# The adaLN rows of the first normalisation computed by halves of the channels in a hybrid RWKV-7 / MLA / MoE block

## What is computed

```python
mod = jax.nn.silu(c) @ w_ada[l] + b_ada[l]                       # (1, 6 * 1024)
sh_m, sc_m, gt_m, sh_f, sc_f, gt_f = jnp.split(mod, 6, axis=-1)
h = modulate(rmsnorm(x, g_norm_mix[l]), sh_m, sc_m)              # h * (1 + sc_m) + sh_m
z = h @ w_in[l]
...
w_log = -jax.nn.softplus(-(w0 + jnp.tanh(zw) @ w_decay_up)) - 0.5
a = jax.nn.sigmoid(a0 + za @ w_a_up)
```

## Time and profile before

| | us |
|---|---|
| median of 3 runs | 1513.24 |
| lowest and highest run | 1509.96, 1517.48 |
| profiled execution, its own time | 1519.26 |
| its span | 1517.4 |
| PE busy | 1384.3 (91%) |
| DVE busy | 761.0 (50%) |
| ACT busy | 492.4 (32%) |
| POOL busy | 313.4 (21%) |

### The profile page before, as it was taken

The page is one execution under the profiler, slowest core; times in us unless marked ns, Lnnn a source line. Parts: engine busy times, 40 slices in busy tenths (PEclk is TensorE's granted clock), DMA queues, the critical chain, the costliest instruction groups (busy, mean ns, idle before and its releaser), DMA issues. The chain is left out here.

```text
span 1517.4 us, 32870 instructions
## 1 busy us (share of the span) xinstructions
PE 1384.3 (91%) x14305; PEld 997.9 (66%) x14305; DVE 761.0 (50%) x1139; ACT 492.4 (32%) x891; POOL 313.4 (21%) x327
## 2 busy tenths in 40 slices
PE   3899999986999998799989999999996799999996
PEld 2687777735899998677767888787885333332332
DVE  3715676766677665445647555656455422111111
ACT  4433232263344443444435444413111111111110
POOL 0002221205556552011110000000000123332323
PEclk8899999997999999899999999999997699999998
DMA  9761322270000001750003113514227899999992
GB/s 373 272 187 45 91 76 63 80 269 2 4 4 4 4 11 39 208 201 15 15 15 153 56 56 110 195 46 167 84 83 275 352 345 399 382 402 376 398 364 56
DMA packets 74956, 238.20 MB, mean 157 GB/s; under 512 B 12216, under 2 KB 37304, under 8 KB 58048
## 3 DMA queue, kind: packets, MB, share of 16 engines
q1 hardware_dynamic: 63872, 219.31, 38.7%
q0 software_dynamic: 10944, 16.82, 4.6%
HBM read 207.74 MB, written 51.40 MB: 171 GB/s over the span
## 5 line engine op out<-in xcount | busy, mean ns | idle before, releaser
L3050 PE MATMUL ps<-gu,xT 128*32 128x512 f32 x1296 | 178.3, 609 | 5.0 <-DMA gu<-w_e_up 3.5
L3266 DVE TENSOR_TENSOR sg<-sg,ps 128x256 f32<-128x256 f32 x25 | 10.5, 421 | 206.6 <-ACT sg L3136 206.6
L3050 PEld LDWEIGHTS ps<-gu,xT 128*32 128x32 f32 x1296 | 46.8, 112 | 98.9 <-issue 95.3
L2937 POOL DMA_INDIRECT out<-YTM,home x48 | 75.2, 1566 | 169.3 <-DVE YTM L3275 162.0
L354 PE MATMUL ps<-hh,wr_h 128*128 128x512 f32 x224 | 94.0, 420 | 4.5 <-DVE hl L350 3.8
L355 PE MATMUL ps<-hl,wr_h 128*128 128x512 f32 x224 | 89.4, 399 | 0.0
L356 PE MATMUL ps<-hh,wr_l 128*128 128x512 f32 x224 | 89.4, 399 | 0.0
L3068 PE MATMUL ps<-dn,hidT 128*32 128x512 f32 x648 | 86.7, 592 | 0.5 <-ACT hidT L3140 0.5
L2117 DVE TENSOR_REDUCE nmax<-ps 128x1 f32<-128x896 f32 (+4 forms) x64 | 45.8, 753 | 72.3 <-PE ps L2015 71.7
L2955 POOL MEMSET xg<- 128x3072 f32 x1 | 2.7, 2657 | 366.5 <-PE ps L2442 366.5
L1285 POOL TENSOR_TENSOR off<-mats,cst 128x256 f32<-128x256 f32 x80 | 66.7, 851 | 50.9 <-PE ps L1707 50.6
(11 more groups left out here) (440 smaller groups left out, 3432.8 us busy)
## 6 DMA issues: line engine op xcount, KB each, us to landing
gu<-w_e_gate SPq DMA_DIRECT2D x29, 1024.0 KB, 17.4
gu<-w_e_up SPq DMA_DIRECT2D x29, 1024.0 KB, 23.5
dn<-w_e_down SPq DMA_DIRECT2D x29, 1024.0 KB, 18.0
wbuf<-w_ada SPq DMA_DIRECT2D x16, 1024.0 KB, 12.9
wbuf<-w_ada SPq DMA_DIRECT2D x16, 512.0 KB, 4.6
wraws<-w_gates SPq DMA_DIRECT2D x16, 512.0 KB, 4.9
wr<-w_rwkv SPq DMA_DIRECT2D x14, 512.0 KB, 3.6
qk_cols<-YTM SPq DMA_DIRECT2D x8, 768.0 KB, 5.3
```

The source lines that it names most:

```text
L2937: pool.indirect_dma_start(out=out[0], out_offset=bass.IndirectOffsetOnAxis(ap=col.bitcast(u32), axis=0), in_=yo[:, buf], in_offset=None, b ...
L3050: last = nc.tensor.matmul(ps[part, GB[b]], xT[:, b, k, part], gu[expert(m, c_) % WB][:, :, k], start=(k == 0), stop=(k == KD - 1))
```

## The change

**Rows of the first modulation.** A new class `HalfRows` takes the place of `Rows` for the first pair (not for `rows4` and `rows2`). Channels are split in two halves of 512 columns. Half h has the shift columns in strip 32h and the scale columns in strip 64 + 32h of its own PSUM bank (6 or 5), so a piece is 512 KB and costs two matmul calls on two strips 64 apart; there are 16 pieces. The bias comes into PSUM as a product of a row of ones with the bias row (`biased`). ACT copies the shift strip out (`shift_row`), DVE the scale strip with the gain (`scale_row`).

**Order.** All eight tiles of `x` are loaded first (tile 7 into the space of `zm`), then bias and gains, then half 0 of the rows, the first two weight tiles, half 1, and the rest. Only the identity and one row of the constants come early. Squares of tiles 1 and 3 move to DVE, roots go by two tiles. PE starts with half 0's bias product, runs half 0's pieces among the transposes, then channel block 0, half 1's bias product and first four pieces, block 1, the other four pieces, block 2, the second turn of the rows, and blocks 3 to 7.

**Phases 2 and 3.** `up_projections` has the token halves outside and the two row groups inside; its weights are loaded some 200 us earlier, and the table `sel` is waited for together with them. The four stores of `rows2` move to the start of phase 3, and DVE waits for its own last bias add instead. The setting up of `S` and `headrk` moves from DVE to POOL, behind `prepare(0)`.

```diff
+        class HalfRows:
...
+            def part(self, h, a):
+                return slice(64 * a + 32 * h, 64 * a + 32 * h + 32)
...
+            def load_bias(self, sp):
+                sp.dma_start(self.bias[0:1], b_ada[:, 0:2 * D]).then_inc(self.b_in, 16)
+                for h in range(2):
+                    sp.dma_start(self.gains[self.part(h, 1)],
+                                 g_norm_mix[:, h * 512:(h + 1) * 512].broadcast_to([32, 512])).then_inc(self.b_in, 16)
...
+            def biased(self, pe, h):
+                pe.wait_ge(self.b_in, 48)
+                for a in range(2):
+                    nc.tensor.matmul(ps[self.part(h, a), self.banks[h]], C("ones")[0:1, 0:32],
+                                     self.bias[0:1, a * D + h * 512:a * D + (h + 1) * 512], start=True, stop=False,
+                                     skip_group_check=True)
...
+            def products(self, pe, h, k):
...
+                pe.wait_ge(self.w_in[h][k], 16)
+                for a in range(2):
+                    m = nc.tensor.matmul(ps[self.part(h, a), self.banks[h]], self.crep[:, k], self.piece(h, k)[:, a],
+                                         start=False, stop=(k == KD - 1), skip_group_check=True)
+                m.then_inc(self.mm, 1)
...
+                    squares(0)
+                    roots(0)
+                    squares(2)
+                    roots(1)
+                    squares(4)
+                    turned(0)
+                    squares(5)
+                    roots(2)
+                    for t in (1, 2):
+                        turned(t)
+                    for t in (6, 7):
                         squares(t)
...
+                    pe.wait_ge(const_in, 32)
+                    rows0.biased(pe, 0)
+                    for t in range(NT):
+                        row_transposes(t)
+                        if t >= NT - 3:
+                            for k in range(2 * (t - NT + 3), 2 * (t - NT + 3) + 2 if t < NT - 1 else KD):
+                                rows0.products(pe, 0, k)
+                    row_columns(0)
+                    channel(0)
+                    rows0.biased(pe, 1)
+                    for k in range(CT):
+                        rows0.products(pe, 1, k)
+                    channel(1)
+                    for k in range(CT, KD):
+                        rows0.products(pe, 1, k)
+                    channel(2)
+                    row_columns(1)
+                    for k in range(3, KD):
+                        channel(k)
...
-                    rows2.store(sp, 1)
...
-                        for j, (w, src, done) in enumerate(((wup[0:64], Z(WA)[0:64], dec),
-                                                            (wup[64:128], Z(WA)[64:128], a_done))):
-                            if c_:
-                                pe.wait_ge(done, c_)
-                            for n in range(2):
+                        for n in range(2):
+                            for j, (w, src, done) in enumerate(((wup[0:64], Z(WA)[0:64], dec),
+                                                                (wup[64:128], Z(WA)[64:128], a_done))):
+                                if c_ and n == 0:
+                                    pe.wait_ge(done, c_)
...
+                    nc.gpsimd.memset(S[:], 0.0).then_inc(init, 1)
+                    for c_ in range(CT):
+                        nc.gpsimd.tensor_scalar(headrk[:, c_], C("heads"), PC("r_k", c_), None, ALU.mult)\
+                          .then_inc(init, 1)
```

More of the change, by code:

```diff
@@ L536, in _, with roots @@
                     nc.scalar.activation(csig[:], ccol[:], ACT.Sigmoid).then_inc(c_sig, 1)
+                    act.wait_ge(const_in, 32)
+                    nc.scalar.activation(mcol[:, 0, 0, 0:1], C("ident")[:, 0:1], ACT.Sqrt)
                     def squares(t):
[L539 to L546, removed]
+                        act.wait_ge(x_in[t], 16)
+                        n = sum(i not in ON_DVE for i in range(t))
+                        if n:
+                            act.wait_ge(ssq, n)
+                        nc.scalar.activation(tmp[:], rows_of(t), ACT.Square, accum_out=ss[:, t:t + 1]).then_inc(ssq, 1)
+                    def roots(two):
+                        cols = slice(2 * two, 2 * two + 2)
+                        act.wait_ge(rstd, 2 * two + 1)
                         nc.scalar.activation(rs[:, cols], rs[:, cols], ACT.Sqrt).then_inc(root, 1)
@@ L553, in turned @@
                           .then_inc(xn_a, 1)
-                    for t in range(4):
+                    squares(0)
[9 more added lines that the diff above has]
+                    for t in (6, 7):
                         squares(t)
[L556 to L559, removed]
+                    roots(3)
+                    for t in range(3, NT):
                         turned(t)
-                    squares(XT)
-                    roots(1)
-                    for t in range(4, NT):
-                        turned(t)
+                    rows0.shift_row(act, 0)
                     for c_ in range(2):
                         weights(c_, 16)
-                    act.wait_ge(mcol_s, 1)
                     act.wait_ge(xn_a, NT)
@@ L721, in _ @@
                         low_part(hl[:, k], xn(k), hh[:, k]).then_inc(h_lo, 1)
+                    squares(1)
+                    roots(0)
+                    for t in (0, 1):
+                        scale_rows(t)
+                    squares(3)
+                    roots(1)
+                    for t in (2, 3):
+                        scale_rows(t)
+                        turned(t - 2)
+                    turned(2)
+                    roots(2)
+                    for t in (4, 5):
+                        scale_rows(t)
+                    for t in (3, 4):
+                        turned(t)
+                    roots(3)
+                    for t in (6, 7):
+                        scale_rows(t)
+                    for t in (5, 6, 7):
+                        turned(t)
+                    rows0.scale_row(dve, 0)
+                    columns(0)
+                    weights(0, 1)
+                    dve.wait_ge(mcol_s, 1)
+                    dve.wait_ge(xn_a, NT)
+                    dve.wait_ge(xn_d, NT)
+                    modulated(0)
+                    weights(1, 2)
+                    for k in range(1, CT):
+                        modulated(k)
+                    nc.vector.memset(zT[:, 0:2, 0:1], 0.0).then_inc(zero, 1)
+                    rows0.scale_row(dve, 1)
+                    columns(1)
+                    dve.wait_ge(const_in, 48)
+                    dve.wait_ge(mcol_s, 2)
+                    for k in range(CT, KD):
+                        modulated(k)
                     dve.wait_ge(wm_hi, 1)
@@ L1549, in _ @@
                     exponents(0)
-                    nc.vector.memset(S[:], 0.0).then_inc(init, 1)
-                    for c_ in range(CT):
-                        nc.vector.tensor_scalar(headrk[:, c_], C("heads"), PC("r_k", c_), None, ALU.mult)\
-                          .then_inc(init, 1)
                     for j in PERIODS:
```

184 lines of the change are left out of this document (98 added, 86 removed).

## The result

Over five runs each the change takes 1525.91 us (1524.22 to 1530.74) and the kernel before 1517.01 (1509.96 to 1519.96); the ratio is 1.0065, 95% interval 1.0043 to 1.0086. I forecast 1514.3 and a range of 1506 to 1520. Of the 11.6 us by which that missed, 3.8 are the base: I had added to the median of three runs, 1513.24, and over five runs the kernel before takes 1517.01. The other 7.8 are the change. The profiled execution of the change took 1525.91 us with a span of 1524.1.

What follows compares the result with a forecast made beforehand. PE was taken as full from 56 us to phase 1's end, with DMA, then small steps, bounding before. Terms +1.5 - 1.1 + 0.7 = +1.1 us on the median of 1513.24 gave 1514.3 us, range 1506 to 1520.

Steps and rivals of the forecast that it cites:

- Gains and the first matmul: Start of phase 1: gains land at 15.6 us, and PE's first instruction, the bias product, waits for them.
- Half 0: Phase 1, first half of the rows: transposes and half pieces at 0.86 us each, its products ending at 35.5 us.
- First block: Phase 1: ACT and DVE steps of 6.2 us after the half's end, first channel block at 41.7, 8.1 us earlier.
- Behind it: Phase 1, busy PE after the first block: added work brings the latent products to 76.5 against 75.05, +1.5 us.
- The stall ahead of block 4: Phase 1: PE waits 0.9 us because 3.6 us of preparation stand against block 3's 2.8.
- Up-projections, 0: Up-projections: the two row groups already run side by side, 2.00 us per 8 instructions, so the new order gains 0.
- Stores, -1.1: Border of phases 2 and 3: moving the four stores out of the phase saves 1.1 us.
- POOL, +0.7: Start of phase 3: POOL's added setup, some 1.5 us, delays DVE's steps by 0.7 us, bounds 0 to +2.0.
- the upper end: Start of phase 3: the bound of +2.0 us, if DVE waits for all of POOL's added work.
- The sum,: Whole kernel: +1.5 for phase 1, -1.1 for stores, +0.7 for POOL's setup, in all +1.1 us.
- that rival: Half pieces in phase 1: two idle strips let TensorE's clock fall to 1.2 GHz, giving 1525 us; chance 0.10.
- Rival one: Phase 1: half pieces cost 0.43, or transposes don't wait for gains; 1507 us either way, 1501 with both; chance 0.12.

Runs made afterwards that it cites:

- mended: The change with its late constants load cut in two (rows 1 to 15 and 16 to 127), DVE waiting for both: 1517.63 us, 0.9994 of the kernel before.

## Why the prediction was wrong

- **The step that failed** is the one that is not in it: the late load of the constants. I counted the constants only at the start, where they shrink "680 to 69 KB" ahead of the gains, and never asked what the other 611 KB cost where they went. The wait `const_in 48` on DVE ahead of block 4 had no term, and the sentence "The stores of `h` and the weights of later tiles have tens of us of slack" was true for queues that drain at 400 GB/s. The load alone costs 9.6 us on the kernel before (1527.98 to 1518.34); the change lost 8.9 against before and 8.3 against itself with the load cut in two (1525.91 to 1517.63).
- **Gains and the first matmul:** forecast 15.6, measured 16.28. Right.
- **Half 0:** forecast to end at 35.5, measured 36.8 (33.13 + 3.63). Late by the gains' 0.7 and by small steps; one sum in it was off by 0.2 (23.6 + 1.1 + 2.6 is 27.3, not 27.1). A half piece at 0.86: measured 3.63 for four, as forecast.
- **First block:** forecast 41.7, measured 42.68 and, mended, 42.15.
- **Behind it:** forecast 76.5 for the first latent product. Mended, it came at 76.64. Before, it starts at 74.89; the 75.05 of my sum is the end of the last matmul ahead of it, so +1.5 stands against +1.75 measured from start to start. The stall ahead of block 4 was forecast at 0.9 and took 0.95.
- **Up-projections, 0:** right, 1.99 against 2.00 at the full clock. PE's wait at the start of phase 2, from which I took nothing, is still there (1.95 us before, 1.78 after).
- **Stores, -1.1:** right. PE's wait at the border of phases 2 and 3 fell from 2.51 us (before its first instruction there, at 343.30) to 1.36 (at 354.20).
- **POOL, +0.7:** too much. The first exponents on ACT lie 6.22 us behind DVE's last add (347.15 from 340.93) before and 5.23 after (358.21 from 352.98), so that stores and setting up together bring -1.0. POOL's added work was also mis-sized: 3.8 us (0.52 + 3.25) and not 1.5. DVE's steps beside POOL's took 2.24, 0.82 and 0.68 us after, 2.49, 0.69 and 0.69 before: none waited for all of POOL's work, which would have cost 2. PE's first instruction that waits for `init`, which POOL now gives, came 6.31 us behind DVE's last add (359.29 from 352.98) and 7.54 before (348.47 from 340.93), so the longer work did no harm there either. The Trainium skill, "SBUF — State Buffer", section "Summary: rules for kernel authors", says that when a DVE instruction with two SBUF inputs meets a GpSimd one that reads SBUF, the second to issue waits until the first is finished. I had read that as giving the upper end, but it speaks of one instruction and not of all of POOL's work. For the first instruction the trace agrees: of DVE's four scans the first took 1.24 us and the others 0.39 to 0.44, and it ended 0.28 us after POOL's product (355.73 from 355.45). Before, it took 1.54 us and also ended 0.28 after it (344.85 from 344.56). The step at 356.76 fits less well: it took only 0.13 us longer than before, although a product of POOL's ran until 357.27 beside it. The first wait was there in both kernels; what was wrong is the step from it to 2 us.

```profile
352.98 0.69 DVE L339 TENSOR_TENSOR YTM<-YTM,ps 128x512 f32<-128x512 f32 x1
354.49 2.24 DVE L1560 TENSOR_TENSOR_SCAN cum<-cst,lw 128x128 f32<-128x128 f32 x4 [0.83 <-DVEq L1113]
356.76 0.82 DVE L1565 TENSOR_TENSOR ex<-cum,lw 128x512 f32<-128x512 f32 x1
357.50 0.68 DVE L1568 TENSOR_TENSOR ex<-cum 128x512 f32<-128x512 f32 x1
```

```profile
354.18 1.27 POOL L1354 TENSOR_TENSOR rk<-zT 128x512 f32<-128x512 f32 x1 [30.56 <-POOLq L1113]
355.39 0.52 POOL L1400 MEMSET S<- 128x512 f32 x1
355.90 3.25 POOL L1402 TENSOR_SCALAR zT<-cst,pc 128x128 f32<-128x128 f32 x4
```

- **The sum,** +1.1 us, stands against -0.9 for the mended change by its ratio, with an interval of -2.7 to +0.8, so it lies 0.3 above that interval; its parts in the profiles are +1.75 at the first latent product and -1.0 at the start of phase 3. The terms that I had were right to 2 us.
- **The rivals:** the clock stayed full among half 1's pieces (1.00 from 50 to 56 us), so that rival is out; its 1525 agrees with the measured 1525.9 by chance. Rival one named the right place for a gain (the wait for the gains), but the change does not take it. None of them held the cause. Phase 1 ends 11.0 us later than before; of these 8.9 are left in the medians and 6.7 between the two profiled spans, since the later phases vary by a few microseconds.

## What to carry to other kernels

When a transfer is cut to leave out what was already loaded, look at the row count that is left, and follow the rest of it to where it went: 127 rows took 25 us where 128 or 15 + 112 cost nothing that could be measured. The queue that stood still here had two waits behind it; taking away the one that the profile showed brought up the other, so mend the transfer and not the wait. And time in which an engine waits for data is free: put small products there (on two strips they also kept the clock at 1.00, on four they did not), and give the first matmul no wait that its data don't need. An earlier start counts only until the next landing: look at what else comes just in time before you add it up.

## What the runs showed of the hardware

- A DMA of 127 rows of 4.9 KB ran at 25 GB/s, and SP stood over the next DMAs of 64 KB for 21.93 us (30.03 on the kernel before), although fifteen engines had nothing to do. What in the queue holds SP there was not tried.
- Products of 32 output columns on two strips of 512, one half piece every 1.35 us with 0.3 us of idle time between, ran at a granted clock of 1.00, and so did the first block behind them. As four strips of 256 the clock was 0.50 from 30 to 36 us. It had fallen before PE's wait of 1.92 us there (the wait ended at 31.65): the bias product at 28.95 already took 0.78 us in place of 0.63. From 24 to 29 us, at 1.00 in both kernels, PE was busy for 2.50 us on four strips, in pieces with 0.5 to 0.7 us of idle time between them, and for 4.84 on two. So the long wait is not what made it fall in that run; no run varies PE's idle time alone.
- A float32 product with 32 output columns costs by its columns and not by the number of strips beside it: four half pieces take 3.63 us on two strips of 512 and 1.93 on four strips of 256.
